# The gate columns' sigmoid: taken where they are read back, not where they are stored

## The reference, cut to what matters

```
z = h @ w_in
z_mla, z_rwkv, z_gate = jnp.split(z, [MLA_COLS, MLA_COLS + RWKV_COLS], axis=-1)
y_a = mla_branch(z_mla, ...)
y_b = rwkv7_branch(z_rwkv, ...)
gate_a, gate_b = jnp.split(jax.nn.sigmoid(z_gate), 2, axis=-1)
x = x + (gate_a * y_a + gate_b * y_b) @ w_out
```

## Time and profile before

| | |
|---|---|
| median of 3 runs | 3272.35 us (3272.25 to 3274.73) |
| profiled execution, its own time | 3269.93 us |
| span of its instructions | 3268.1 us |
| TensorE busy | 2955.8 us (90%) |
| VectorE busy | 1438.5 us (44%) |
| ScalarE busy | 750.8 us (23%) |
| mean granted TensorE clock | 0.942 |

### The profile page before, as it was taken

One profiled execution on the slowest core, in us unless ns is written; L12 is line 12 of the kernel. 1 busy time (PEld: TensorE's weight loads), 2 busy tenths in 40 slices (PEclk: granted clock), 3 DMA queues, 4 the chain that ended last, 5 costly groups with the idle time before them and its releaser, 6 DMA issues.

```text
span 3268.1 us, 38655 instructions
## 1 busy us (share of the span) xinstructions
PE 2955.8 (90%) x16560; PEld 2415.6 (74%) x16560; DVE 1438.5 (44%) x2059; ACT 750.8 (23%) x1000; POOL 390.1 (12%) x288
## 2 busy tenths in 40 slices
PE   5879899999999499988888699979999999999886
PEld 4767788888888387867666477768778888888765
DVE  6973432332323434444444755665343333333434
ACT  4132311121111311034332232231221110111312
POOL 0000110010000200000002501113211111111201
PEclk9989999999999799989999798889999999999998
DMA  4141111111111032244446211325111111111101
GB/s 154 34 110 39 58 52 39 52 52 52 39 52 39 26 94 105 84 136 127 141 128 181 78 40 66 104 84 174 52 38 41 52 52 52 39 52 52 65 13 52
DMA packets 221274, 236.97 MB, mean 73 GB/s; under 512 B 60112, under 2 KB 174672, under 8 KB 220208
## 3 DMA queue, kind: packets, MB, share of 16 engines
q1 hardware_dynamic: 221104, 234.49, 22.6%
HBM read 178.50 MB, written 56.20 MB: 72 GB/s over the span
## 4 chain that ended last, share of the span: by engine, by line
PE 80%; DVE 12%; ACT 3%; issue 2%; DMA 1%; POOL 1%; SPq 1%; POOLq 0%; DVEq 0%; ACTq 0%
PE bank L610 20%; PE bank L611 20%; PE bank L612 20%; PE bank L2404 2%; PE bank L2424 2%; PE bank L1751 2%; PE bank L1752 2%; PE bank L1753 2%; PE bank L2599 1%; PE bank L2412 1%; DVE op_lo L192 1%; PE bank L1936 1%; DVE tmp L182 1%; PE bank L1970 1%; PE bank L629 1%
## 5 line engine op out<-in xcount | busy, mean ns | idle before, releaser
L610 PE MATMUL bank<-op_hi,w_hi 128*128 128x512 f32 x1952 | 765.9, 392 | 27.3 <-DVE ple_tmp L182 17.6
L611 PE MATMUL bank<-op_lo,w_hi 128*128 128x512 f32 x1952 | 764.0, 391 | 0.0
L612 PE MATMUL bank<-op_hi,w_lo 128*128 128x512 f32 x1952 | 763.3, 391 | 0.0
L610 PEld LDWEIGHTS bank<-op_hi,w_hi 128*128 128x128 f32 x1952 | 369.5, 189 | 107.2 <-issue 23.6
L612 PEld LDWEIGHTS bank<-op_hi,w_lo 128*128 128x128 f32 x1952 | 369.3, 189 | 77.4
L611 PEld LDWEIGHTS bank<-op_lo,w_hi 128*128 128x128 f32 x1952 | 369.6, 189 | 76.7
L610 PE MATMUL bank<-f_hi,w_hi 128*128 128x512 f32 x864 | 337.8, 391 | 12.3 <-DVE hT L182 9.1
L182 DVE TENSOR_TENSOR w_lo<-w_raw,w_hi 128x2048 fp32r<-128x2048 f32 (+2 forms) x116 | 256.5, 2213 | 199.8 <-ACT w_hi L419 195.8
L611 PE MATMUL bank<-f_lo,w_hi 128*128 128x512 f32 x864 | 337.1, 390 | 0.0
L612 PE MATMUL bank<-f_hi,w_lo 128*128 128x512 f32 x864 | 337.1, 390 | 0.0
L182 DVE TENSOR_TENSOR hT<-hT,bank 128x512 f32<-128x512 f32 x256 | 170.4, 685 | 367.1 <-PE bank L612 367.1
(11 more groups left out here) (444 smaller groups left out, 3791.6 us busy)
## 6 DMA issues: line engine op xcount, KB each, us to landing
record<-record_scratch SPq DMA_DIRECT2D x16, 1024.0 KB, 5.3
w_raw<-in_w_ffn_up SPq DMA_DIRECT2D x16, 1024.0 KB, 5.2
w_raw<-in_w_ffn_down SPq DMA_DIRECT2D x16, 1024.0 KB, 5.0
w_raw<-in_w_in SPq DMA_DIRECT2D x13, 1024.0 KB, 5.7
w_raw<-in_w_gate SPq DMA_DIRECT2D x11, 1024.0 KB, 5.2
w_raw<-in_w_up SPq DMA_DIRECT2D x11, 1024.0 KB, 5.2
w_raw<-in_w_down SPq DMA_DIRECT2D x10, 1024.0 KB, 4.9
w_raw<-in_w_in SPq DMA_DIRECT2D x17, 512.0 KB, 4.3
```

The lines of the kernel that those rows point to most:

```text
L610: t.matmul(ps[:], hi[:, k, wc], x[0][:, k, xc], start=k == 0, stop=False)
L611: t.matmul(ps[:], hi[:, k, wc], x[1][:, (k + turn) % KD, xc], start=False, stop=False)
L612: last = t.matmul(ps[:], lo[:, k, wc], x[0][:, k, xc], start=False, stop=k == kt - 1)
```

## The change

The sigmoid of the gate columns moves. In the first stage SyncE stores each gate tile as VectorE left it, and waits for VectorE instead of ScalarE. In the mix ScalarE takes the sigmoid in place, in the ring buffer, and VectorE waits for that instead of for the transfer. ScalarE runs four tiles ahead: tiles 0 to 3 first, tiles 4 to 19 each after VectorE is done with the tile four places earlier, and tiles 20 to 31 one before each of the first twelve `op_hi` copies. The split of `wt_o` block 2 moves from before the tiles to between tiles 11 and 12, that of block 3 behind tile 19.

```diff
     def gates_sync(q):
         def end(n):
             i, half = gate_tiles[n]
-            q.wait_ge(*Sg.A.of("gate", n))
+            q.wait_ge(*Sg.V.of("gate", n))
             q.dma_start(z_tile(Z_GATE + i * P, half), mem.z_out[half][:]).then_inc(*d_z[half].up(n, by=16))
...
     def gates_scalar(s):
...
-        def end(n):
-            i, half = gate_tiles[n]
-            s.wait_ge(*Sg.V.of("gate", n))
-            s.activation(mem.z_out[half][:], mem.z_out[half][:], ACT.Sigmoid).then_inc(*Sg.A.up("gate", n))
-
-        return gate_steps(idle, split, idle, end)
+        return gate_steps(idle, split, idle, idle)
...
-    NG = len(mem.gate_in)
+    NG, GATE_AHEAD = len(mem.gate_in), 4
...
     def mix2_scalar(s):
...
-        wt_o.split_hi(s, 2)
+
+        def sigmoid(n):
+            s.wait_ge(*d_gin[n % NG].of(n))
+            g = mem.gate_in[n % NG][:]
+            s.activation(g, g, ACT.Sigmoid).then_inc(*A.up("gate", n))
+
+        for n in range(GATE_AHEAD):
+            sigmoid(n)
+        for n in range(GATE_AHEAD, 16 + GATE_AHEAD):
+            s.wait_ge(*V.of("gated", n - GATE_AHEAD))
+            if n == 8 + GATE_AHEAD:
+                wt_o.split_hi(s, 2)
+            sigmoid(n)
+            yield
         wt_o.split_hi(s, 3)
         for n, (i, half) in enumerate(tiles16):
             if n == 12:
                 wt3.split_hi(s, 0)
+            if n + 16 + GATE_AHEAD < 32:
+                sigmoid(n + 16 + GATE_AHEAD)
             s.wait_ge(*V.of("mixed", i, half))
             s.activation(op2[0][:, i, hs(half)], mixed[:, i, hs(half)], ACT.Copy).then_inc(*A.up("hi", i, half))
             yield
...
         def gated(n, dst, name):
             w, i, half = gated16[n]
             v.wait_ge(*T.of(name, i, half))
-            v.wait_ge(*d_gin[n % NG].of(n))
+            v.wait_ge(*A.of("gate", n))
```

## The result

| | before | after |
|---|---|---|
| median of 19 runs | 3269.05 us (3259.39 to 3274.73) | 3275.49 us (3271.85 to 3284.37) |
| ratio | | 1.0024, 95% interval 1.0015 to 1.0033 |
| profiled execution, its own time | 3269.93 us | 3273.18 us |
| span | 3268.1 us | 3271.4 us |

The interval is a loss of 4.9 to 10.8 us. The forecast time of 3274.4 us is 1.1 us off, but the forecast *change* was +2.0 us, and the medians show +6.4: the before of the prediction, the median of three runs, lay 3.3 us above that of nineteen. One later run of the kernel before, 5000.92 us long at a granted clock of 0.552, is left out of every comparison.

A forecast was written before the change was run, and what follows sets the result against it. TensorE was taken as the bound (80% of the chain, ScalarE 3%). Terms 2.0 - 3.5 + 1.4 + 2.1 = +2.0 us gave 3271.9, plus 2.4 for the runs' median: 3274.4 us, range 3269 to 3279.

The forecast's parts named there:

- The start: Start of the gate stage: two exposed table loads, partly offset by an earlier store, start TensorE 2.0 us later.
- The end of pair 0's front: Gate weight block: `w_lo` released 2.0 us earlier and 1.5 us of clock regained, -3.5 us; bounds -2.0 and -3.6.
- The clock term: Behind the shortened stall at pair 0's end: granted clock 1.00 instead of 0.56, so 1.5 us come back.
- The fronts of pairs 1 to 3: A load before each first sigmoid delays TensorE's bank: 0.2, 0.6 and 0.6, sum +1.4 us; bounds 0 and +2.1.
- The mix: First output-projection block: late sigmoids 30 and 31 delay the weight split, TensorE waits 2.1 us; bounds 0 and +3.6.
- The sum: Whole kernel: 2.0 - 3.5 + 1.4 + 2.1 = +2.0 us against the profiled execution's 3269.93.
- Both clock terms wrong: Clock falls behind both the 1.6 us stall and the new mix stall: +5.0, 3277.4 us; chance 0.15.
- A switch costs more than its load: At table switches, a drain as long as the load: +5.2 on top, 3279.6 us; chance 0.02.
- The last two gates come late: At sigmoid 30 in the mix, load 30 lands later: +2.5 and 1.5 of clock, 3278.4 us; chance 0.07.
- Nothing is exposed: First load hidden, banks free in time, load 30 sooner: -2.9, 3269.5 us; chance 0.08.
- Faster: ScalarE's freed 35.6 us shorten other stalls too, 8.5 us more than counted: 3264 us; chance 0.03.

The follow-up runs named there:

- 1: Kernel after with gates stored without their sigmoid and none taken later, the mix as before: 3274.26 us, 1.0019 against the kernel before.
- 3: Kernel after with the split of wt3 block 0 moved ahead of the sigmoids of gate tiles 30 and 31: 3271.61 us, 1.0014 against before.
- 5: Kernel after with the wt3 split moved ahead and one one-column sigmoid at the start of the first front: 3270.75 us, 1.0006 against before.
- experiments 4: Kernel after with the wt3 split moved ahead and four one-column sigmoids loading the table early, at the start and in three backs: 3266.39 us, 0.9992.
- experiment 10: Repeat timing of the kernel after with the wt3 split moved ahead and four one-column sigmoids loading the table early: 3266.03 us, 0.9990 against before.
- 6: Kernel after with the wt3 split moved ahead and one-column sigmoids only in the backs of pairs 0 to 2: 3268.89 us, 0.9994 against before.
- experiment 9: Kernel before with only gate tiles 3 to 6 stored without their sigmoid, which is taken nowhere: 3262.89 us, 0.9980 against before.
- 12: Kernel after with gates stored without sigmoid, none taken in the mix, and four one-column sigmoids loading the table early: 3265.45 us, 0.9980 against before.

## Why the prediction was partly right

**The start, +2.0 forecast.** Right in mechanism and size: both loads exposed, 2.3 us in the traces. The operations on `lo_rank` and `g_rank` ended at 1420.0 and 1422.4 (forecast 1419.5 and 1421.8), half a microsecond late, because the wait for `chunk_mask` ended at 1417.64 and not at 1417.2. TensorE's stall there is 8.2 us by mean in the four traces that store as before, 10.5 in the five with two exposed loads and 7.7 in the five with the early store and the table loaded ahead: the loads cost 2.7 us and the earlier store gives 0.5 back.

**The end of pair 0's front, -3.5 forecast.** Right: -2.0 from the release and -1.6 from the clock in the traces, and -5.6 +- 1.2 in the timed kernel that has this alone. The clock term, taken from the nearest stall, held in every trace: over 3.5 us, from 1.4 us behind the stall's end, the granted clock was 0.56 to 0.62 in the three traces with the long stall and 1.00 in the eleven with the short one. The stretch shows it too: 35.4 us for the stretch instead of 37.0, six times out of six (36.05, with pair 1's load, in the other five).

**The fronts of pairs 1 to 3, +1.4 forecast, bound +2.1: this step failed.** TensorE's rows show +0.65, +1.12 and +1.12, together 2.9 us, the stretches 3.1, the timed pairs 4.3 and 5.3. The wrong row was read: the prediction named the right product but took its time from the row at 1557.72, with 0.7 us of slack behind the sigmoid of the earlier trace rows. Each of these products has two rows, and that is a second one. The product that takes the bank starts at 1557.20, with 0.2 us of slack, in the trace of the kernel before:

```profile
1557.20 0.69 PE L1898 MATMUL bank<-lo_rank,w2a 64*128 64x512 f32 x1
```

So the term for pairs 2 and 3 was 0.6 where 1.1 was measured. The placing of the loads was right: behind the wait in pairs 2 and 3 (0.49 us idle ahead of them, as in the row of the kernel after above), inside it in pair 1, where 0.65 us were lost and not 0.2. The upper bound repeated the fault, since it let the idle half microsecond ahead of a load count as cover in all three pairs.

**The mix, +2.1 forecast, bound +3.6.** The chain came as written: load 30 landed at 2269.9 (forecast 2270.3), `w_hi` at 2272.02 (2272.5), `w_lo` done at 2276.2 (2276.7), a stall of 1.6 us here and up to 2.5 in the other traces. What was left out is what comes behind it: the mix is 2.4 us longer, and the later stages another 1.0, 3.4 in all; that lies inside the bound, but what makes the extra stays open. In this trace the clock did not fall right behind the stall (1.00 from 2276.30 on), so the extra is not the fall right behind the stall that the bound and the rival named. In the traces, moving the split ahead of the wait takes all of it back.

**The sum** missed by two terms, 1.7 us in the fronts and 1.3 in and behind the mix: +5.1 by the traces instead of +2.0. That the forecast time is only 1.1 us off is luck: the change was forecast 4.4 us too small, and the median that it was added to stood 3.3 too high. Another 2.6 us of the measured 7.7 +- 0.7 stays open. The kernels with exposed loads in the fronts (1, 3, 5, after) stand 2.0 to 3.5 us above their trace sums, the others 1.6 above to 1.9 below, so it may belong to the same step; that it is the clock, which in more executions falls in a stage that these loads have shifted, is argued and not shown: each kernel has one or two traces, and the mean granted clock of the runs is 0.940 both for the kernel after and for the one before. Another share of executions with the longer attention, told of below, would do as well and is no better shown.

**The rivals.** *Both clock terms wrong* fell: one of them held in every trace. *A switch costs more than its load* fell. In the kernel after the load at the start ends at 1418.92 and its activation starts at 1418.94; the Trainium skill (page ScalarE: Activation LUTs, section What ACT_TABLE_LOAD costs) counts about 1.38 us of drain for a switch, and no row here shows one. *The last two gates come late*: load 30 landed at 2269.9, where 2270.3 was forecast. *Nothing is exposed* and *Faster* fell. The prediction gave slower by over 0.2% a chance of 0.1 and expected no change that could be measured; the two timings of the kernel after, 1.0024 and 1.0025, lie just beyond that bound.

**A version that might beat both** would store only gate tiles 3 to 6 without their sigmoid and take these four in the first half of the mix, where ScalarE is idle. It was not run. The mended kernel (experiments 4 and 10) is 10 us faster than the kernel after and 0.1% faster than the one before.

## What to carry to other kernels

Taking a function off an engine also takes away its table: look at which function stood last ahead of each wait, because its load was paid in the idle time ahead of the wait, and the next function's load, which is placed behind the wait, is not. A one-column activation ahead of the wait puts the load back there. And where new work that waits for a late transfer is put in an engine's queue, move what the critical engine needs next ahead of it; the slack of a handed-on bank is to be read from the first row of the product that takes it.

## What the runs showed of the hardware

The same program varies by 24 us (3254.95 to 3278.54 in 11 runs of the kernel before), and the traces show one place where they part by 6 us: late in the attention, in identical code, four of the fourteen traces (experiments 5, 6, 9 and 12) took 434.8 to 435.1 us from the stage's end to the mix, where the others took 428.8 to 429.3. The same stretch of work in experiment 9 and in experiment 10 (stretch, length, busy by engine, granted clock, DMA share, GB/s):

```profile
2140.80:2144.80 4.00, 4.00 (x31) 3.56 (x32) 1.65 (x5) 0.56 (x2) 0.00 (x0) 0.64 0.43 167
2144.80:2148.80 4.00, 4.00 (x41) 3.26 (x40) 1.27 (x4) 0.60 (x2) 0.00 (x0) 0.51 0.02 4
```

```profile
2138.50:2142.50 4.00, 4.00 (x65) 3.53 (x65) 2.08 (x6) 1.05 (x3) 0.00 (x0) 1.00 0.38 144
2142.50:2146.50 4.00, 4.00 (x21) 2.84 (x22) 3.27 (x9) 0.56 (x2) 0.00 (x0) 1.00 0.00 0
```

The clock was at its lower level (0.5 of full speed, 1.2 GHz) for most of 8 us in the one and at full speed in the other, with TensorE busy all the time in both. The four traces that lost 6 us here got 1.1 us back in the mix and 1.2 behind it, so 3.6 us remain. What decides between the two isn't shown: none of the four kernels has a second trace. A difference of 3 us between two kernels can be hidden or feigned by such a place, so the worth of an edit is seen only over many runs, or stretch by stretch.
